# Feed-forward products from the unscaled residual, and GpSimd's past taps paced by weight units, in a two-layer retention and convolution decoder step

## The chip, the cores and the metric

One core of one Trainium2 chip runs the whole program. The metric is the device time of one execution in microseconds. The engines are TensorE (PE; its weight loads PEld), VectorE (DVE), ScalarE (ACT), GpSimd (POOL) and SyncE (SP), each with its own instruction queue; they meet at semaphores.

## What is computed

Two trunk layers over 320 tokens (256 of a prompt, 8 x 8 of a decoding batch), width 1024, all in fp32:

```python
h = rms_norm(x, g_mix_pre); proj = h @ w_in          # q, k, v, g_ret, ca, cb, ga, gb
# retention: rope(q, k), chunkwise state, layer norm, silu(g_ret) * o, @ w_ret_out
# convolution: u = ca * sigmoid(cb), depthwise, 31 taps, layer norm, silu, @ w_conv_out
merged = sigmoid(ga + b_ga) * y_ret + sigmoid(gb + b_gb) * y_conv
x = x + rms_norm(merged @ w_o, g_mix_post)
h2 = rms_norm(x, g_ffn_pre)
f = (silu(h2 @ w_ffn_gate) * (h2 @ w_ffn_up)) @ w_ffn_down
x = x + rms_norm(f, g_ffn_post)
```

`rms_norm` divides each token by the root of its mean square. The new states of retention and convolution are outputs too.

## The kernel before

Tokens lie along the free axis, features on the partitions (8 tiles of 128x320). Each product is made in units: a unit is 8 tiles of 128x128 weights, 512 KB, one output tile of 128x320. fp32 is split in two fp32r halves: ScalarE copies the weights to `whi` and VectorE makes `wlo = w - whi` (L1025, the helper `lower`, called by `split`), and TensorE does three products per tile (L415 to L417 in `unit`, `bank` in PSUM). A layer has 180 units: 16 of the convolution inputs (CIN), 4 heads of 12, 8 of the gate gb, 24 of ga and the retention output (RET), 8 convolution output, 8 `w_o`, 44 feed-forward gate and up alternating (GU, from U_GU = 112), 24 down. Four ring slots hold weights; `split(l, u)` prepares unit u + 3 (AHEAD = 3), once unit u - 1 is done.

The order on each engine is written out by hand:

- `normalised` (VectorE, L1038) makes h = x times gain times rstd, ScalarE copies the upper half `hhi` (`halves_of_h`, L894), VectorE the lower half `hlo`. `first_units` (TensorE, L435 to L437) then does the first three units of a stage together, K-step by K-step, as the halves come: 8 steps of 9 matmuls. `rsqrt` (ScalarE) is Ln (L774) then Exp (L781) of the mean square, which TensorE sums over the partitions with `ones_d` (`stat`, L468; L449 and L454 for squares of products). `keep_clock(n)` issues n products whose result nobody reads (L444).
- `log_exp_table` (L770) loads by name a table of ScalarE that has both Ln and Exp. Other loads are placed by the compiler.
- The depthwise convolution of the prompt is 124 taps of two VectorE instructions each (128x256, L1056 for a pair's first tap, L1060 for the others), spread by hand over units: CIN_TAPS, FIRST_HEAD_TAPS, HEAD_TAPS, GB_TAPS, RET_TAPS say how many taps follow the split of each unit, by layer.
- The sample's convolution is GpSimd's: `past_taps` (L272 product, L275 addition, 30 taps, 60 instructions; here 128x512 or less) over the stored rows, `new_taps` (L289, L291). Its queue is: past taps of layer 0, store of cs_out, new taps, then the state stores and loads of each head (L299, L257), later the past taps of layer 1 during layer 0's feed-forward, from the third gated product on (FFN_FIRST).
- A head's retention is done in two parts: `early` in its own units, `late` in the next head's (or gb's) units 0 to 7, between the K-steps (j, k). UPDATE_AT holds the eight places of the state update products (L580, two at a time), QUERY_AT those of the state reading products (L563), which wait for the state's load. `update` (VectorE, L1091) takes a product's bank into the state; `aux_free` lets a product reuse one of three banks only when the product three before it has been read. So the products at (5, 5) wait for update 12, the first of the two that follow the split of unit 5.
- `post` (VectorE) copies the product, waits for the rstd, then adds it to x in four groups of two tiles (L1374, L1376); ScalarE squares each tile of x (L992) for the next norm.
- In the feed-forward, ScalarE takes the sigmoid of the gate bank (L793), VectorE multiplies bank and sigmoid (L1393) and then with the up bank (L1399), ScalarE and VectorE make the halves for the down product (L999, L1025).

## Time and profile before

| | us |
|---|---|
| median of 3 runs | 1566.42 (1566.14 to 1571.51) |
| the profiled execution | 1567.79 |
| its span | 1566.0 |
| TensorE busy | 1513.0 (97%), 9840 instructions |
| VectorE busy | 1107.8 (71%) |
| ScalarE busy | 674.4 (43%) |
| GpSimd busy | 287.5 (18%) |
| chain that ended last, by engine | PE 79%, DVE 14%, ACT 3% |

The mean granted clock of TensorE is 0.99 of 2.4 GHz. TensorE's busy time contains the fillers of `keep_clock`, and matmuls overlap, so a busy TensorE can still hold time that isn't needed. A matmul of the main product is listed with 0.31 us, and the next one starts 0.15 us behind it.

### The profile page before, as it was taken

To read this page: it belongs to the slowest core of one execution; us is meant where nothing else is said; L and a number is where in the kernel's file an instruction comes from. 1 tells how busy PE (TensorE), PEld (TensorE's weight loads), DVE (VectorE), ACT (ScalarE), POOL (GpSimd) and SP (SyncE) were. 2 spreads that over 40 slices of the span, in tenths; PEclk is the share of its full clock that TensorE was granted. 3 is DMA by queue.
4 is the path that set the end of the run, shared out by engine and by line. 5 is a ranking of instruction groups with operands and counts; after the bars stand their busy time and mean duration, and the time that the engine had idled before them with its cause. 6 is when DMAs were issued, how large, how long until landed. Compare 5 with 4: busy or idle time off the path is not lost.

```text
span 1566.0 us, 25591 instructions
## 1 busy us (share of the span) xinstructions
PE 1513.0 (97%) x9840; PEld 1399.5 (89%) x9840; DVE 1107.8 (71%) x1735; ACT 674.4 (43%) x993; POOL 287.5 (18%) x257
## 2 busy tenths in 40 slices
PE   6999999999999999999999999999999999999997
PEld 5997878687999999999999978788789998999997
DVE  6699978977757567654456988989685665655544
ACT  4333434355355354334343334344464544443433
POOL 6974000011110029910000400101002000000000
PEclk9999999999999999999999999999999999999999
DMA  6554755647444434444444555658554342544443
GB/s 255 175 193 158 275 201 216 229 175 256 135 149 147 157 110 146 157 148 158 156 152 158 195 207 216 245 183 311 180 184 161 135 148 68 175 148 148 155 156 117
DMA packets 64540, 275.48 MB, mean 176 GB/s; under 512 B 7232, under 2 KB 7232, under 8 KB 55232
## 3 DMA queue, kind: packets, MB, share of 16 engines
q1 hardware_dynamic: 52560, 192.17, 35.8%
q0 software_dynamic: 11888, 82.04, 13.9%
q8 instruction: 62, 1.02, 0.3%
q14 instruction: 30, 0.25, 0.0%
HBM read 230.30 MB, written 43.89 MB: 175 GB/s over the span
## 4 chain that ended last, share of the span: by engine, by line
PE 79%; DVE 14%; ACT 3%; issue 1%; POOL 1%; DVEq 0%; ACTq 0%
PE bank L415 23%; PE bank L417 22%; PE bank L416 22%; DVE acc L1060 4%; DVE wlo L1025 3%; PE bank L602 2%; DVE state L1091 1%; PE bank L580 1%; DVE tmp L1080 1%; PE bank L563 1%; PE bank L516 1%; DVE x L1376 1%; ACT L770 1%; DVE tmp L1374 1%; PE bank L545 1%
## 5 line engine op out<-in xcount | busy, mean ns | idle before, releaser
L415 PE MATMUL bank<-hhi,whi 128*128 128x320 f32 x2016 | 654.5, 325 | 1.6 <-DVE wlo L1025 1.6
L417 PE MATMUL bank<-hhi,wlo 128*128 128x320 f32 x2016 | 625.2, 310 | 0.0
L416 PE MATMUL bank<-hlo,whi 128*128 128x320 f32 x2016 | 624.8, 310 | 0.0
L1025 DVE TENSOR_TENSOR wlo<-wring,whi 128x1024 fp32r<-128x1024 f32 x363 | 470.4, 1297 | 217.0 <-ACT whi L763 194.5
L415 PEld LDWEIGHTS bank<-hhi,whi 128*128 128x128 f32 x2016 | 380.8, 189 | 33.6 <-issue 29.3
L416 PEld LDWEIGHTS bank<-hlo,whi 128*128 128x128 f32 x2016 | 381.1, 189 | 8.6 <-issue 7.7
L763 ACT ACTIVATE whi<-wring 128x1024 fp32r<-128x1024 f32 x264 | 278.1, 1055 | 241.4 <-PE bank L417 239.1
L417 PEld LDWEIGHTS bank<-hhi,wlo 128*128 128x128 f32 x2016 | 380.5, 189 | 0.0
L1060 DVE SCALAR_TENSOR_TENSOR acc<-up,par,acc 128x256 f32<-128x256 f32 x480 | 211.1, 507 | 0.2
L789 ACT ACTIVATE whi<-wring 128x1024 fp32r<-128x1024 f32 x96 | 101.2, 1054 | 73.3 <-PE bank L417 72.0
L793 ACT ACTIVATE sig<-bank 128x320 f32<-128x320 f32 x92 | 40.2, 437 | 199.6 <-PE bank L417 187.2
L415 PE MATMUL bank<-fhi,whi 128*128 128x320 f32 x352 | 110.4, 314 | 0.0
L417 PE MATMUL bank<-fhi,wlo 128*128 128x320 f32 x352 | 108.5, 308 | 0.0
L416 PE MATMUL bank<-flo,whi 128*128 128x320 f32 x352 | 108.5, 308 | 0.0
L1091 DVE SCALAR_TENSOR_TENSOR state<-state,con,bank 128x512 f32<-128x512 f32 x128 | 89.8, 744 | 11.4 <-PE bank L580 10.3
L299 POOL DMA_DIRECT2D rs_out<-state x32 | 17.3, 541 | 390.1 <-DVE state L1091 390.1
L392 POOL DMA_DIRECT2D par<-params x2 | 1.2, 576 | 465.0 <-DVE acc L1368 465.0
L415 PE MATMUL bank<-ghi,whi 128*128 128x320 f32 x256 | 78.8, 308 | 2.4 <-DVE glo L1025 2.4
L416 PE MATMUL bank<-glo,whi 128*128 128x320 f32 x256 | 78.8, 308 | 0.0
L417 PE MATMUL bank<-ghi,wlo 128*128 128x320 f32 x256 | 78.7, 307 | 0.0
L1393 DVE TENSOR_TENSOR tmp<-bank,sig 128x320 f32<-128x320 f32 x44 | 21.6, 492 | 70.5 <-ACT sig L793 70.5
L416 PEld LDWEIGHTS bank<-flo,whi 128*128 128x128 f32 x352 | 66.1, 188 | 0.6
(157 smaller groups left out, 1948.1 us busy)
## 6 DMA issues: line engine op xcount, KB each, us to landing
wring<-w SPq DMA_DIRECT2D x364, 512.0 KB, 3.7
state<-r_in POOLq DMA_DIRECT2D x32, 1024.0 KB, 7.6
rs_out<-state POOLq DMA_DIRECT2D x32, 1024.0 KB, 5.0
rp_out<-pst POOLq DMA_DIRECT2D x8, 512.0 KB, 8.4
us<-c_in POOLq DMA_DIRECT2D x2, 1216.0 KB, 5.7
cs_out<-us POOLq DMA_DIRECT2D x2, 1216.0 KB, 9.4
cp_out<-up POOLq DMA_DIRECT2D x2, 1144.0 KB, 5.9
con<-consts POOLq DMA_DIRECT2D x1, 1420.0 KB, 9.3
```

Source lines behind the costliest of these rows:

```text
L299: pool.dma_start(rs_out[H * QUADS + q], state[q % 2][:, :, :]).then_inc(r_stored[q % 2], 16)
L415: pe.matmul(bank[g][:, 0:T], whi[j][:, k, :], hi, start=start and k == 0, stop=False)
L416: pe.matmul(bank[g][:, 0:T], whi[j][:, k, :], lo, start=False, stop=False)
L417: mm = pe.matmul(bank[g][:, 0:T], wlo[j][:, k, :], hi, start=False, stop=stop and k == n - 1)
L602: mm = pe.matmul(aux[pos % 3][:, :], kdec[:, c, d * P:(d + 1) * P], vtok[:, c, :], start=(c == 0), stop=(c == 1))
L763: act.activation(whi[s][:, :, :], wring[s][:, :, :], ACT.Copy).then_inc(hi_done, 1)
L789: act.activation(whi[s][:, :, :], wring[s][:, :, :], ACT.Copy).then_inc(hi_done, 1)
L793: act.activation(dst, src, ACT.Sigmoid).then_inc(sig_done, 1)
L1025: return dve.tensor_tensor(dst, value, hi.bitcast(F32), ALU.subtract)
L1060: dve.scalar_tensor_tensor(out=out, in0=src, scalar=tap, in1=out, op0=ALU.mult, op1=ALU.add).then_inc(conv_step, 1)
L1091: dve.scalar_tensor_tensor(out=st, in0=st, scalar=con[:, ds(hd + C_CD, 1)], in1=aux[pos % 3][:, :], op0=ALU.mult, op1=ALU.add).then_inc(dv ...
L1393: dve.tensor_tensor(tmp[:, n % 4, :], bank[b][:, 0:T], sig[:, n % 4, :], ALU.mult).then_inc(ffn_step, 1)
```

## The change

1. Feed-forward entrance: the units work on x times gain, without rstd. ScalarE makes `hhi` straight from x as its groups come (MIX_GROUPS, two of one tile, three of two), VectorE `hlo` (`x_low`). The mean square runs meanwhile: squares are added in halves (`add_squares`), and TensorE sums four in place of eight, inside `first_units`. The split of unit U_GU stands ahead of the wait for the mixer's rstd, that of U_GU + 1 behind the feed-forward's. keep_clock(20) and keep_clock(12) become one keep_clock(12).
2. In each feed-forward step VectorE multiplies the gate bank by rstd, ScalarE takes Silu of that, VectorE multiplies the up bank by rstd and then both with each other.
3. Start of layer 0: squares of x are added in halves, four sums in place of eight, 18 fillers before them; the named table load goes; GpSimd's first past taps wait for all eight `hlo`.
4. GpSimd's past taps of layer 1 wait, each, for a unit: the first for 20 units of the stage, the others spread over 42.
5. `first_updates` puts the updates 0, 1, 8, 9, 12, 13 and the token statistics ahead of the split of their unit; UPDATE_AT (4, 7) becomes (4, 5).
6. Tap lists of layer 0: 8 taps in CIN (0 before), 10 in head 0 (16), 23 in head 1 (27), 21 in gb (20), 8 in RET (7).

```diff
-CIN_TAPS = (0, 2)
-FIRST_HEAD_TAPS = ((1, 2, 1, 1, 1, 2, 2, 1, 1, 1, 1, 2), (2, 2, 2, 2, 2, 2, 2, 1, 1, 1, 1, 2))
-HEAD_TAPS = ((7, 0, 3, 0, 4, 1, 5, 4, 3, 0, 0, 0), (7, 0, 3, 0, 3, 1, 4, 3, 2, 0, 0, 0))
-GB_TAPS = ((6, 0, 3, 3, 3, 1, 4, 0), (5, 0, 3, 3, 2, 1, 3, 0))
-RET_TAPS = ((1, 2, 2, 2, 0, 0), (1, 2, 2, 1, 0, 0))
-FFN_FIRST = 3
+CIN_TAPS = ((1, 1, 1, 1, 2, 2), (2, 2, 2, 2, 2, 2))
+FIRST_HEAD_TAPS = ((1, 1, 1, 1, 1, 1, 1, 1, 1, 0, 0, 1), (2, 2, 2, 2, 2, 2, 2, 1, 1, 1, 1, 2))
+HEAD_TAPS = ((5, 0, 3, 0, 3, 1, 5, 3, 3, 0, 0, 0), (7, 0, 3, 0, 4, 1, 5, 4, 3, 0, 0, 0), (7, 0, 3, 0, 3, 1, 4, 3, 2, 0, 0, 0))
+GB_TAPS = ((6, 0, 3, 3, 3, 2, 4, 0), (5, 0, 3, 3, 2, 1, 3, 0))
+RET_TAPS = ((2, 2, 2, 2, 0, 0), (1, 2, 2, 1, 0, 0))
+FFN_FIRST, TAP_UNITS = 20, 42
-UPDATE_AT = ((1, 0), (1, 3), (1, 5), (1, 7), (4, 3), (4, 7), (5, 3), (5, 5))
+UPDATE_AT = ((1, 0), (1, 3), (1, 5), (1, 7), (4, 3), (4, 5), (5, 3), (5, 5))
...
+                    if paced:
+
+                        pool.wait_ge(unit_done, (l - 1) * UNITS + (U_GU + FFN_FIRST + k * TAP_UNITS // PAD))
...
+                    pool.wait_ge(h_ready, KT)
                     past_taps(0, past0, stap, par[:, G_CB:G_CW], par[:, G_CW:NPAR])
...
+                if l == 0:
+                    keep_clock(18)
+                    for k in (0, 1, 4, 5):
+                        pe.wait_ge(x_halves, k // 4 + 1)
+                        mm = pe.matmul(X[:, 0:T], ones_d[:, :], sq8[:, k, :], start=(k == 0), stop=(k == 5))
...
-                keep_clock(20)
...
+                def both_halves(k):
+
+                    if k == 5:
+                        half_mean(0)
+                    if k == 6:
+                        half_mean(1).then_inc(stat_done, 1)
+
+                first_units(l, U_GU // RING, lambda k: h_read(l, 8 + k), between=both_halves)
...
-            log_exp_table()
...
+                split(l, U_GU)
                 act.wait_ge(stat_done, l * STATS + (ST_POST + 1))
                 rsqrt(l, X[:, 0:T], ST_POST, RS_POST)
...
+                for i, (k0, n) in enumerate(MIX_GROUPS):
+                    act.wait_ge(post_step, l * POSTS + (2 * i + 2))
+                    for k in range(k0, k0 + n):
+                        act.activation(hhi[:, k, :], x[:, k, :], ACT.Copy, scale=g_(G_FFNPRE + k)).then_inc(h_hi, 1)
+                    for k in range(k0, k0 + n):
+                        act.activation(sq8[:, k, :], x[:, k, :], ACT.Square).then_inc(sq_done, 1)
...
-                    gemm(l, U_GU + 2 * n)
-                    sigmoid(sig[:, n % 4, :], bank[(2 * n) % 4][:, 0:T])
+                    act.wait_ge(ffn_step, l * (2 * FT) + (2 * n + 1))
+                    act.activation(sig[:, n % 4, :], sig[:, n % 4, :], ACT.Silu).then_inc(sig_done, 1)
...
+            def first_updates(l, hd, j):
+
                 if j in (1, 4, 5):
                     q = (1, 4, 5).index(j)
+                    for i in range(2):
                         update(l, hd, (0, 8, 12)[q] + i)
+                if j == 5:
+                    token_stats(l, hd, 1, range(2, 3))
+
+                    dve.wait_ge(bn_done, (l * HEADS + hd) * 3 + 3)
+                if j == 6:
+                    token_shift(l, hd, 1, slice(2, 3))
...
+                for i, (k, n) in enumerate(MIX_GROUPS):
+                    x_group(l, 2 * i, k, n)
+                    for low in ((), (0,), (1,), (2, 3), (4, 5, 6, 7))[i]:
+                        if low == 7:
+                            add_squares(0)
+                            add_squares(1)
+                        x_low(low)
...
+                    dve.tensor_tensor(sig[:, n % 4, :], bank[b][:, 0:T], rstd[:, :], ALU.mult).then_inc(ffn_step, 1)
...
+                    dve.tensor_tensor(tmp[:, n % 4, :], bank[b + 1][:, 0:T], rstd[:, :], ALU.mult).then_inc(ffn_up, 1)
+                    dve.wait_ge(ffn_up, l * FT + (n + 1))
+                    dve.wait_ge(sig_done, l * SIGS + (SIG_GATE + n + 1))
+                    dve.tensor_tensor(tmp[:, n % 4, :], tmp[:, n % 4, :], sig[:, n % 4, :], ALU.mult).then_inc(ffn_step, 1)
```

## Rows read from the trace of the kernel before

**Rows 1.** Table by stages (stretch, length; busy us of PE, PEld, DVE, ACT, POOL; clock, DMA).

```profile
45.00:130.00 85.00, 84.95 (x583) 84.39 (x582) 66.69 (x88) 31.70 (x46) 71.94 (x56) 1.00 0.52 181
...
200.00:269.00 69.00, 66.32 (x407) 54.49 (x406) 60.44 (x119) 29.02 (x47) 4.80 (x9) 0.98 0.60 221
...
540.50:565.00 24.50, 23.21 (x155) 20.86 (x154) 15.12 (x26) 12.15 (x25) 0.00 (x0) 1.00 0.12 42
565.00:710.00 145.00, 145.00 (x990) 145.00 (x990) 94.26 (x108) 59.76 (x86) 90.42 (x60) 1.00 0.45 152
```

**Rows 2.** Waits of TensorE: who waited for whom, us, times, longest.

```profile
PE bank L580 <- DVE state L1091: 16.2, 17, 2.1
```

**Rows 3.** Table by stages, the half-clock stretches of layer 0's heads.

```profile
173.90:177.30 3.40, 3.40 (x15) 3.40 (x15) 2.79 (x8) 1.84 (x5) 1.05 (x2) 0.50 0.42 163
...
310.40:317.20 6.80, 6.56 (x24) 6.16 (x25) 5.55 (x12) 2.58 (x5) 1.05 (x2) 0.50 0.63 212
```

**Rows 4.** Timeline of TensorE (start, us, engine, line, operation, idle before): products of state updates.

```profile
242.02 0.69 PE L580 MATMUL bank<-vst,kst 32*128 32x512 f32 x2 [2.09 <-DVE state L1091]
...
1012.32 0.50 PE L580 MATMUL bank<-vst,kst 32*128 32x512 f32 x2 [1.30 <-DVE state L1091]
```

**Rows 5.** Timeline of all engines, start of layer 0; two rows of VectorE's.

```profile
9.76 1.28 ACT L770 ACT_TABLE_LOAD   x1
...
11.05 2.95 ACT L913 ACTIVATE whi<-wring 128x1024 fp32r<-128x1024 f32 x3
...
14.97 0.53 ACT L774 ACTIVATE lnv<-bank,eps 128x320 f32<-128x320 f32 x1 [0.97 <-PE bank L468]
...
21.08 1.56 DVE L1043 SCALAR_TENSOR_TENSOR acc<-x,par,rstd 128x320 f32<-128x320 f32 x1
...
21.30 0.60 PE L435 MATMUL bank<-hhi,whi 128*128 128x320 f32 x1 [3.69 <-DVE hlo L1025]
...
89.68 2.34 DVE L1056 TENSOR_SCALAR acc<-up,par 128x256 f32<-128x256 f32 x2
...
105.95 1.67 DVE L1080 TENSOR_TENSOR tmp<-bank,con 128x320 f32<-128x320 f32 x4
```

**Rows 6.** Timeline at the feed-forward's entrance, layer 0.

```profile
543.08 0.83 DVE L1374 TENSOR_TENSOR tmp<-acc,rstd 128x640 f32<-128x640 f32 x1 [1.37 <-ACT rstd L781]
...
552.62 1.48 DVE L1043 SCALAR_TENSOR_TENSOR acc<-x,par,rstd 128x320 f32<-128x320 f32 x3 [3.07 <-ACT rstd L781]
...
554.64 0.38 PE L435 MATMUL bank<-hhi,whi 128*128 128x320 f32 x1 [0.52 <-DVE hlo L1025]
```

**Rows 7.** Timeline of VectorE in head 2, units 4 and 5.

```profile
234.11 2.80 DVE L1091 SCALAR_TENSOR_TENSOR state<-state,con,bank 128x512 f32<-128x512 f32 x4
236.83 3.25 DVE L1060 SCALAR_TENSOR_TENSOR acc<-up,par,acc 128x256 f32<-128x256 f32 x8
240.00 1.22 DVE L1025 TENSOR_TENSOR wlo<-wring,whi 128x1024 fp32r<-128x1024 f32 x1
241.13 1.41 DVE L1091 SCALAR_TENSOR_TENSOR state<-state,con,bank 128x512 f32<-128x512 f32 x2
```

**Rows 8.** Timelines of GpSimd and TensorE, head 0 to head 1; DMA issues there.

```profile
105.90 0.53 POOL L360 DMA_DIRECT2D cs_out<-us  x1
...
133.93 1.33 POOL L291 TENSOR_TENSOR acc<-us,stap 128x512 f32<-128x512 f32 x1
...
148.39 0.59 POOL L299 DMA_DIRECT2D rs_out<-state  x1 [13.14 <-DVE state L1091]
...
153.64 0.54 POOL L257 DMA_DIRECT2D state<-r_in  x1 [1.75 <-DMA rs_out<-state]
...
state<-r_in POOLq DMA_DIRECT2D x2, 1024.0 KB, 7.7
...
161.97 1.05 PE L563 MATMUL bank<-state,qz 128*16 128x512 f32 x8
```

**Rows 9.** Timeline of TensorE at the mean of the convolution, layer 0.

```profile
415.33 0.81 PE L695 MATMUL bank<-pairs,ones_d 128*128 128x320 f32 x2 [1.59 <-POOL pairs L371]
```

More of the change, by code:

```diff
@@ L261, in window, with past_taps @@
                 return buf[:, :, :, t0:t0 + n]
-            def past_taps(l, past, ptap, bias, weights):
+            def past_taps(l, past, ptap, bias, weights, paced=False):
                 weights = weights.rearrange("p (n k) -> p n k", n=KT)
@@ L439, in first_units @@
                             mm.then_inc(unit_done, 1)
+                    if between is not None:
+                        between(k)
             def keep_clock(n):
@@ L1208, in head @@
             def head(l, hd, first):
-                taps = (FIRST_HEAD_TAPS if first else HEAD_TAPS)[l]
+                taps = FIRST_HEAD_TAPS[l] if first else HEAD_TAPS[2 if l else min(hd - 1, 1)]
                 for j in range(HEAD_UNITS):
-                    if j == 1 and not first:
-                        update(l, hd - 1, 0)
-                        update(l, hd - 1, 1)
-                    if j == 6 and not first:
-                        token_shift(l, hd - 1, 1, slice(2, 3))
+                    if not first:
+                        first_updates(l, hd - 1, j)
                     split(l, U_HEAD + j, hd)
@@ L1282, in _ @@
                 for n in range(KT):
-                    if n == 1:
-                        update(l, last, 0)
-                        update(l, last, 1)
-                    if n == 6:
-                        token_shift(l, last, 1, slice(2, 3))
+                    first_updates(l, last, n)
                     split(l, U_GB + n)
@@ L1368, in post @@
                         dve.tensor_scalar(acc[:, n, :], bank[n % 4][:, 0:T], g_(gain + n), None, ALU.mult).then_inc(y_copied, 1)
+                    if sub == 0:
+                        split(l, U_GU)
                     dve.wait_ge(rstd_done, l * RSTDS + (rs + 1))
                     dve.wait_ge(y_copied, l * 16 + (8 * sub + 8))
-                    scale = rstd[:, :].rearrange("p (o t) -> p o t", o=1).to_broadcast([P, 2, T])
-                    for n in range(0, KT, 2):
-                        y = tmp[:, n % 4:n % 4 + 2, :]
-                        dve.tensor_tensor(y, acc[:, n:n + 2, :], scale, ALU.mult).then_inc(post_step, 1)
-                        dve.wait_ge(post_step, l * POSTS + (8 * sub + n + 1))
-                        dve.tensor_tensor(x[:, n:n + 2, :], x[:, n:n + 2, :], y, ALU.add).then_inc(post_step, 1)
@@ L1378, in _, with x_group @@
-                post(0, RS_POST, SQ_POST, G_MIXPOST, U_WO, 1)
-                dve.wait_ge(post_step, l * POSTS + 8)
-                normalised(l, 1, RS_FFN, G_FFNPRE)
+                def x_group(l, step, k, n):
+                    y = tmp[:, k % 4:k % 4 + n, :]
+                    scale = rstd[:, :].rearrange("p (o t) -> p o t", o=1).to_broadcast([P, n, T])
+                    dve.tensor_tensor(y, acc[:, k:k + n, :], scale, ALU.mult).then_inc(post_step, 1)
+                    dve.wait_ge(post_step, l * POSTS + (step + 1))
+                    dve.tensor_tensor(x[:, k:k + n, :], x[:, k:k + n, :], y, ALU.add).then_inc(post_step, 1)
@@ new lines, in x_low, with add_squares @@
+                def x_low(k):
+                    dve.wait_ge(h_hi, l * 16 + (8 + k + 1))
+                    dve.scalar_tensor_tensor(out=hlo[:, k, :], in0=x[:, k, :], scalar=g_(G_FFNPRE + k), in1=hhi[:, k, :].bitcast(F32),
+                                             op0=ALU.mult, op1=ALU.subtract).then_inc(h_ready, 1)
+                def add_squares(i):
+                    dve.wait_ge(sq_done, l * SQS + (SQ_FFN + 4 * i + 4))
+                    dve.tensor_tensor(sq8[:, 4 * i:4 * i + 2, :], sq8[:, 4 * i:4 * i + 2, :], sq8[:, 4 * i + 2:4 * i + 4, :],
+                                      ALU.add).then_inc(sq_halves, 1)
```

101 lines of the change are left out of this document (56 added, 45 removed).

## The prediction

> **What bounds the kernel now.** I read the table by stages first. TensorE is the bound nearly everywhere: it is busy for 84.95 of 85 us in the convolution inputs and the first head, and for all 145 us of a feed-forward stretch [rows 1]. So an edit pays only where TensorE stands still, runs fillers, or runs at its lower clock. The reader is to look for the stretches in which its busy time is short of the stretch: a head loses 2.7 of 69 us, the 24.5 us between the output projection and the first feed-forward units lose 1.3 and hide fillers besides [rows 1]. The waits of TensorE say who ends them: 16.2 us in 17 waits are waits of L580 (the state update product) for the VectorE update L1091 [rows 2]. Then the clock: three stretches of the first layer's heads stand at 0.50, which is 1.2 GHz, two of 3.4 us and one of 6.8 us (the first and the last are shown); in the last a matmul takes 6.56 / 24 = 0.27 us [rows 3], against 145 / 990 = 0.147 in the feed-forward [rows 1]. The timeline ties the second of them to a wait: L580 at 242.02 has stood 2.09 us for VectorE, just where the clock falls [rows 4]. The like wait of the second layer is 1.30 us, and the clock stays up behind it [rows 4].
>
> **The part at the start of layer 0.** Before, GpSimd's 60 past-tap operations run beside `normalised`; a VectorE multiply of 128x320 takes 1.56 us there [rows 5] and 0.49 us without GpSimd (1.48 for three) [rows 6]. The change lets GpSimd begin only when all eight `hlo` are made. With eight steps of about 0.87 us (two such operations, each overlapping its successor a little) the first 96 K-steps of TensorE are then no longer fed by VectorE but by its own rate. The first of them starts 2.0 us behind the rstd, as in the feed-forward (552.62 to 554.64) [rows 6], in place of 5.2 us behind it (rstd 1.1 us after Ln's start at 14.97, first product at 21.30) [rows 5], and the 72 matmuls take 72 x 0.147 = 10.6 us in place of some 18 before (21.30 and eight steps of two operations of 1.56 and like length, less their overlap): the first units end some 10 us sooner, if the rstd comes at its old time. Does it? The 18 fillers and the halved sum bring the sum from 14.9 to about 12, but ScalarE has its three copies (2.95 us behind 9.76, where squares end) in front of Ln in any case, so Ln starts at 12.7 at best [rows 5]. The preload of the table is taken out, and Ln and Exp still need a table: with none to load rstd stands at 13.8, with one load of 1.28 at 15.0, with two (one for Ln, one for Exp, as no line now names a table that has both) at 16.3, against 16.1 before. I take the two loads, since the program asked for that table by name wherever both functions follow each other; so the rstd itself gains nothing.
>
> The trace shows 1.28 us for a load, and the next instruction (11.05) starts directly behind it [rows 5]. The Trainium skill (ScalarE: Activation LUTs, What ACT_TABLE_LOAD costs) adds a drain of 1.38 us to each switch of set, 2.66 us in all; by it the two loads would put the rstd 2.8 us later than I take it. The row shows no such drain, so it counts 1.28 here.
>
> The 10 us don't last. GpSimd's 60 operations are now all in front of the convolution inputs and head 0, where VectorE has also got 8 taps in place of none (6 fewer in head 0, net +2). There VectorE and GpSimd hold each other up: a pair of tap instructions that is 0.8 us alone (3.25 for eight) [rows 7] took 2.34 us at 89.68 [rows 5]. From the last `hlo` (about 24) to the second rope of head 0, which TensorE waits for, VectorE has 20 splits x 1.13, 8 gates of bank times sigmoid at about 0.6, 12 taps x 0.8 and some 3.2 of rope = 40 us of its own. A GpSimd operation in between adds 0.77 (2.34 against 0.8, halved) to 1.07 us (1.56 against 0.49), say 0.95, and 24 to 47 of them meet one (half or all of those that fit): 88 to 109. Before, that rope started at 105.95 [rows 5], just in time for TensorE; TensorE by itself now wants the rope's banks 19 units of 3.52 us behind its 28.6, at 95.5. With rope times of 88 to 109, head 0 ends between 9 us sooner and 3 us later. I take no gain, because VectorE is now loaded throughout, so that nearly each of its operations meets one of GpSimd's.
>
> Behind this is GpSimd's own queue: past taps, the cs_out store (105.90), new taps to 135.3, and only then the state stores and loads [rows 8]. Before, it stood waiting for the store at 148.39. 60 operations from 23.6 at the 1.5 to 1.75 us that contention makes of them end at 114 to 129 instead of 105; 30 us later the stores can start, and the load they release lands 12.9 us behind the store (148.39 to the load at 153.64, and 7.7) while TensorE asks for it 13.6 us behind it (161.97) [rows 8]. So the state comes between on time and 8 us late; I take 2 us. **Start and first head: +2 us, from -9 to +10.**
>
> **Heads.** `first_updates` sets two state updates ahead of the weight split of units 4 and 5, and the product at (4,7) moves to (4,5). The product at (5,5) needs update 12. Before, VectorE does four updates (234.11), eight tap instructions (236.83), the split (240.00, 1.13 to the next), then update 12 (241.13) [rows 7]. Now update 12 comes one split sooner: 1.13 us. Queued behind it is the split itself, whose weights are wanted three units (over 10 us) later, so its delay costs nothing; if VectorE were already 7 us behind, it would cost all of its wait. There are eight such places (three heads and the gb stage of each layer). One tap less at unit 4 of head 1 is 0.8 us more: 8 x 1.13 + 0.8 = 9.8, of 16.2 that there is to get [rows 2]; in the last stage of layer 1 part of it is not there. **-9.5 us, from -5 to -12.**
>
> **Clock.** The idle time at (5,5) in heads 2 and 3 of layer 0 falls from 2.09 to about 1.3 us, after which the trace of layer 1 shows no fall [rows 4]. In 13.6 us at 0.27 in place of 0.147 per matmul TensorE loses 13.6 x 0.45 = 6.1 us [rows 3]. I take 5, since new idle time in head 0 and at its followers may cost one fall. **-5 us, from 0 to -6.**
>
> **Convolution sums.** RET_TAPS and GB_TAPS of layer 0 carry one tap more each; the mean's product L695 already stands 1.59 us for GpSimd's sum of them [rows 9]. One tap of two instructions, 0.8 us: **+0.8** (0 to +2).
>
> **Feed-forward entrance, twice.** Before: rstd of the mixer 543.08, four groups of product and addition at 0.83 each, squares, eight products of the sum, Ln, Exp, normalisation, first product 554.64 [rows 6]. Now hhi = x times gain is made while the groups come. ScalarE's and VectorE's split of unit U_GU lie in front: the first is hidden by the sum's own path, the second ends 0.2 us behind the old start, so groups start at 543.3. Two narrow groups (2 x 0.93), one low part 0.5: first product at 545.7. Then a group of two costs 1.6 and low parts 0.5, so that K-steps 1 and 2 (1.32 us each) wait 0.75 each; from K-step 3 on TensorE is behind and the rest is hidden. The 72 matmuls 10.6, idle 1.5, and four sum products of two passes now inside the units, 4 x 0.54 + 0.5 = 2.6: end 560.4, against 554.64 + 10.6 = 565.2. That is 4.75 us, 9.5 for both layers, less 0.1. Next late is the rstd that the bank readers want: sum at 559.3, Ln, Exp 560.5, split, 1.28 load, VectorE's gate scale at 563, with unit 4 wanted at 564. Just hidden; without that cover each us late costs one. If the waits in the K-steps drop the clock, 3.4 to 6.8 us at 1.2 GHz cost 1.5 to 3 us a layer. **-9.4 us, from -3 to -11.**
>
> In steady state, VectorE gets one 0.49 us operation more per pair of units (gate x rstd, up x rstd, product in place of two): 44 in all, 21.6 us. A pair of units is 7.05 us, and VectorE's is then 2 x 1.13 + 4 x 0.45 = 4.1 and the ping-pong with ScalarE (scale, Silu, half, copy, split, up, product, split) 5.4 us, 6.5 with GpSimd between; hidden, as now [rows 1]. Pacing the 30 taps over 42 units takes contention from a stretch that loses nothing and puts it into the down stage, where it loses nothing either: 0. If VectorE fell more than two units behind, it would cost what the cycle has over 7.05.
>
> The trace shows the 1.56 us for operations that read two SBUF tensors. The Trainium skill (GPSIMD Engine Reference, Key points) says just that: contention with VectorE's instructions that have two SBUF inputs or a 2-port mode. By it the two scalings, one input of which is a bank, run free of GpSimd; were they hit too, the cycle would be 7.4 us and the second half of layer 0's feed-forward lose up to 8 us. The page sides with zero; no row here has such a scaling beside GpSimd in the feed-forward.
>
> **The sum.** +2 - 9.5 - 5 + 0.8 - 9.4 = -21.1 us. The profiled execution took 1567.8 (span 1566.0), so its like would take 1546.7; the median shown is 1.4 lower, which gives 1545.3. I say 1546.
>
> **Rivals.**
> - *The start pays too*: VectorE catches up in head 0 and the stores aren't late, so 8 us of the 10 stay. For: GpSimd has idle stretches of VectorE to run in. Against: the second rope was the point that TensorE just met before. 1546 - 10 = 1536. Chance 0.15.
> - *The waits only move*: u8 to u12 are held by the products before them, or the clock falls at the new gaps. Then the heads give 4 and the clock 0: 1546 + 10.5 = 1556. Chance 0.17.
> - *The stage entrance is all that counts* and head 0's lateness takes what the heads give: -9.4 + 10 - 5 = -4: 1562. Chance 0.09.
> - *GpSimd's queue, slower*: its taps meet a VectorE that is never idle. If each of its operations (0.95) has to let a split (1.13) pass, with the gap it takes 2.15 us; 60 of them from 23.6 end at 152, the stores start at 182, the state lands at 195, 33 us late for head 1, where the reordered updates hold up the splits too. The rest gives 23: 1566 + 10 = 1576. It decides from an end of the past taps at 142 on, where the lateness is 23. Against: VectorE must idle where TensorE bounds. Chance 0.04.
> - *It doesn't do what it says*: a table load in each feed-forward step, because Silu's table lacks the copy. 44 x 1.28 on ScalarE per layer would still fit in 7 us: no change of sign. 0.01.
>
> The forecast itself has 0.54. Its own range is 1539 to 1553; with bounds and rivals the range is 1535 to 1560. A measurement of this kernel tells about 0.5% (8 us, below 1558.6) from no change: faster 0.87, same 0.09, slower 0.04.
>
> **What would show it.** L435's first products at about 18 (layer 0) and 9 us sooner than before at both feed-forwards. L580's waits for L1091 from 16.2 to near 7. No half clock between 170 and 320. Past taps ending at 114 to 129 and PE L563 waiting a little for r_in once. ACT table loads in front of both Ln and Exp near 13 and 15. Wrong it would be if TensorE waits for wlo in the feed-forward, or if head 0 starts 10 us sooner and stays so.

## The result and the profile after

The changed kernel takes 1546.86 us (median; 1545.82 to 1548.0) where the kernel before takes 1566.68 on the same chip: a ratio of 0.987, with an interval of 0.9845 to 0.9888. The forecast was 1546. Its span is 1546.2 us against 1566.0. Below stand, for the changed kernel, the page's lines of busy times and of the chain that ended last, the waits of TensorE (who waited for whom, us, times, longest) and the table by stages (columns as in [rows 1]). Its line numbers are shifted: L592, L1125 and L1094 are the state product, the state update and the taps (before L580, L1091, L1060); L445 and L425 the first and the other weight units (L435, L415); L1059 is `lower` (L1025), L1114 the first rotary products (L1080).

```profile
PE 1500.5 (97%) x9772; PEld 1392.2 (90%) x9772; DVE 1143.6 (74%) x1773; ACT 675.4 (44%) x994; POOL 272.0 (18%) x257
PE 80%; DVE 14%; ACT 3%; issue 1%; POOL 1%; DMA 0%; DVEq 0%; ACTq 0%
```

```profile
PE bank L425 <- DVE tmp L1114: 7.8, 2, 4.3
PE bank L592 <- DVE state L1125: 4.8, 10, 1.1
PE bank L445 <- DVE hlo L1059: 4.2, 2, 3.7
...
PE bank L714 <- POOL pairs L382: 3.8, 2, 3.2
```

```profile
45.00:130.00 85.00, 77.19 (x507) 76.36 (x506) 78.06 (x82) 27.71 (x39) 70.18 (x57) 0.96 0.45 154
190.00:267.00 77.00, 75.89 (x474) 63.99 (x474) 67.33 (x133) 32.55 (x53) 4.79 (x9) 0.98 0.60 214
539.50:554.00 14.50, 13.30 (x81) 12.18 (x82) 9.55 (x16) 6.95 (x17) 0.00 (x0) 1.00 0.05 18
554.00:698.00 144.00, 144.00 (x984) 144.00 (x983) 108.70 (x127) 61.85 (x87) 46.93 (x35) 1.00 0.48 152
```

The waits for the state have shrunk from 16.2 us [rows 2] to 4.8. A new wait heads the list: 7.8 us for the rotary products. It lies in the stretch 45 to 130, where TensorE had next to no idle time [rows 1] and now has 7.8 us.

To see where the 19.8 us of span come from, I took from each kernel's timeline of TensorE the start of the last product of a stage, and subtracted that of the kernel before. All kernels of this study stand in one table (us; layer 0 up to the bar). Each row is one execution, the profiled one, and differences of up to 3 us in it can be stretches at half clock that come in one execution and not in another (last section):

| kernel | conv. input | head 0 | gb | RET | first 3 FF units | &#124; gb | conv. output | first 3 FF units, and end |
|---|---|---|---|---|---|---|---|---|
| changed | -9.9 | +1.2 | -9.1 | -6.0 | -11.3 | -16.4 | -14.5 | -19.8 |
| a_no_start | -0.3 | -0.1 | -9.7 | -9.7 | -15.0 | -19.3 | -19.2 | -24.5 |
| a_no_heads | -9.0 | +0.5 | -2.8 | -1.2 | -6.5 | -6.8 | -6.5 | -11.7 |
| a_ffn_alone | -0.1 | +0.1 | 0.0 | 0.0 | -5.3 | -5.6 | -5.6 | -10.9 |
| a_burst | -8.6 | +0.4 | -11.8 | -8.7 | -13.9 | -17.8 | -16.2 | -21.5 |
| a_small_taps | -8.7 | -9.0 | -20.5 | -17.5 | -22.8 | -27.9 | -27.5 | -32.8 |
| a_rope_first | -9.7 | -0.7 | -11.9 | -8.7 | -14.0 | -17.7 | -17.4 | -22.7 |
| b_ret | -10.1 | +2.6 | -10.6 | -10.6 | -15.9 | -20.9 | -20.5 | -25.8 |
| a_combo | -13.5 | -3.5 | -13.2 | -13.2 | -18.6 | -23.7 | -23.3 | -28.6 |
| c_later_taps | -13.5 | -7.8 | -11.2 | -11.2 | -16.5 | -21.3 | -20.9 | -25.4 |
| b_gate_off | +0.3 | +2.0 | -10.3 | -7.0 | -12.3 | -16.3 | -15.9 | -21.2 |
| c_update47 | -9.9 | +1.2 | -9.5 | -6.3 | -11.6 | -16.1 | -15.7 | -21.0 |
| d_spread | -13.5 | -13.8 | -21.9 | -21.9 | -27.2 | -31.8 | -31.4 | -36.7 |

The first row reads as a sum: the start and head 0 cost 1.2, the heads up to gb give 10.3 in layer 0 and 5.1 in layer 1, each feed-forward entrance 5.3, the retention output's stage takes 3.2 and layer 1's stages up to the convolution output take 1.9 back.

**The start.** Timelines of the changed kernel: ScalarE, TensorE's first product, GpSimd's first past tap.

```profile
12.37 1.28 ACT L805 ACT_TABLE_LOAD   x1
13.67 0.53 ACT L805 ACTIVATE lnv<-bank,eps 128x320 f32<-128x320 f32 x1
14.21 1.28 ACT L812 ACT_TABLE_LOAD   x1
15.51 0.47 ACT L812 ACTIVATE rstd<-lnv 128x320 f32<-128x320 f32 x1
...
18.11 0.38 PE L445 MATMUL bank<-hhi,whi 128*128 128x320 f32 x1 [3.66 <-DVE hlo L1059]
...
23.27 1.06 POOL L281 TENSOR_TENSOR past<-us,par 128x512 f32<-128x512 f32 x1 [11.56 <-DVE hlo L1059]
```

Two loads stand in front of Ln and Exp, and the first units still end 9 to 10 us sooner, as the table's first column has it.

**Head 0 of layer 0.** VectorE's timeline, the first matmuls behind TensorE's two waits, and the table by stages behind each.

```profile
88.57 2.08 DVE L1059 TENSOR_TENSOR wlo<-wring,whi 128x1024 fp32r<-128x1024 f32 x1
90.58 2.71 DVE L1094 SCALAR_TENSOR_TENSOR acc<-up,par,acc 128x256 f32<-128x256 f32 x2
93.21 1.67 DVE L1114 TENSOR_TENSOR tmp<-bank,con 128x320 f32<-128x320 f32 x4
...
94.54 0.54 PE L425 MATMUL bank<-hhi,whi 128*128 128x320 f32 x1 [4.28 <-DVE tmp L1114]
...
106.92 0.41 PE L425 MATMUL bank<-hhi,whi 128*128 128x320 f32 x1 [3.54 <-DVE tmp L1114]
```

```profile
94.70:98.10 3.40, 3.40 (x14) 3.40 (x15) 3.40 (x4) 0.00 (x0) 3.24 (x3) 0.50 0.00 0
108.30:111.70 3.40, 3.40 (x15) 3.40 (x14) 3.40 (x5) 0.00 (x0) 3.01 (x6) 0.50 0.10 17
```

Here the start's gain is lost: 4.4 and 3.7 us by the starts of the matmuls, and the clock falls to 1.2 GHz for 3.4 us behind each wait (0.50 in the table), which costs 1.5 us a time. That is the 11.1 us between the first two columns.

**The retention output's first units.** GpSimd's last sum of the convolution, TensorE's product that waits for it, and the stretch behind it in the table by stages.

```profile
406.06 1.72 POOL L382 TENSOR_TENSOR pairs<-pairs 128x320 f32<-128x320 f32 x1
...
407.83 0.81 PE L714 MATMUL bank<-pairs,ones_d 128*128 128x320 f32 x2 [3.22 <-POOL pairs L382]
```

```profile
408.70:412.10 3.40, 3.40 (x15) 3.40 (x14) 0.00 (x0) 0.00 (x0) 0.00 (x0) 0.50 0.42 140
```

The wait was 1.59 us [rows 9]. It is 1.6 us longer, and RET loses 3.2 us in all against gb; the other 1.5 are the half clock. a_no_heads has the same longer wait and no half clock there, and loses 1.6 (-2.8 to -1.2).

**The feed-forward's entrance.** Timeline of the changed kernel.

```profile
539.80 0.38 PE L445 MATMUL bank<-hhi,whi 128*128 128x320 f32 x1 [1.13 <-DVE hlo L1426]
...
541.77 0.41 PE L445 MATMUL bank<-hhi,whi 128*128 128x320 f32 x1 [0.41 <-DVE hlo L1426]
...
554.88 1.28 ACT L1039 ACT_TABLE_LOAD   x1
...
556.04 0.48 DVE L1455 TENSOR_TENSOR sig<-bank,rstd 128x320 f32<-128x320 f32 x1
```

The layer stood 5.99 us ahead at its output projection; with that added the first product is at 545.8 in the time of the kernel before, where the prediction has 545.7.

### The profile page after: what moved, and what is told of

It is laid out like the page before. It is cut to its first block, busy times and chain, and to the rows that moved or that the text cites. A ratio compares the mean times of both kernels' runs of the same rounds, so it can differ in the third digit from the quotient of the medians.

```text
span 1546.2 us, 25486 instructions
## 1 busy us (share of the span) xinstructions
PE 1500.5 (97%) x9772; PEld 1392.2 (90%) x9772; DVE 1143.6 (74%) x1773; ACT 675.4 (44%) x994; POOL 272.0 (18%) x257
## 4 chain that ended last, share of the span: by engine, by line
PE 80%; DVE 14%; ACT 3%; issue 1%; POOL 1%; DMA 0%; DVEq 0%; ACTq 0%
PE bank L425 23%; PE bank L427 22%; PE bank L426 22%; DVE acc L1094 5%; DVE wlo L1059 2%; PE bank L614 2%; DVE state L1125 2%; PE bank L592 1%; PE bank L575 1%; DVE tmp L1114 1%; PE bank L445 1%; PE bank L528 1%; PE bank L447 1%; PE bank L446 1%; PE bank L557 1%
## 5 line engine op out<-in xcount | busy, mean ns | idle before, releaser
L425 PE MATMUL bank<-hhi,whi 128*128 128x320 f32 x2016 | 655.4, 325 | 8.7 <-DVE tmp L1114 7.8
L1059 DVE TENSOR_TENSOR wlo<-wring,whi 128x1024 fp32r<-128x1024 f32 x363 | 479.6, 1323 | 192.3 <-ACT whi L794 178.1
L425 PEld LDWEIGHTS bank<-hhi,whi 128*128 128x128 f32 x2016 | 381.2, 189 | 40.3 <-issue 29.3
L1094 DVE SCALAR_TENSOR_TENSOR acc<-up,par,acc 128x256 f32<-128x256 f32 x480 | 226.4, 536 | 0.2
L425 PE MATMUL bank<-fhi,whi 128*128 128x320 f32 x352 | 110.5, 314 | 0.0
L1125 DVE SCALAR_TENSOR_TENSOR state<-state,con,bank 128x512 f32<-128x512 f32 x128 | 89.4, 739 | 11.2 <-PE bank L592 10.3
L425 PE MATMUL bank<-ghi,whi 128*128 128x320 f32 x256 | 78.9, 308 | 2.4 <-DVE glo L1059 2.4
L1039 ACT ACTIVATE sig<-sig 128x320 f32<-128x320 f32 x44 | 20.8, 472 | 123.9 <-DVE sig L1455 123.9
L425 PEld LDWEIGHTS bank<-fhi,whi 128*128 128x128 f32 x352 | 66.1, 188 | 0.6
L427 PEld LDWEIGHTS bank<-fhi,wlo 128*128 128x128 f32 x352 | 66.1, 188 | 0.0
```

Of the source, the lines that this page charges most:

```text
L425: pe.matmul(bank[g][:, 0:T], whi[j][:, k, :], hi, start=start and k == 0, stop=False)
L427: mm = pe.matmul(bank[g][:, 0:T], wlo[j][:, k, :], hi, start=False, stop=stop and k == n - 1)
L1039: act.activation(sig[:, n % 4, :], sig[:, n % 4, :], ACT.Silu).then_inc(sig_done, 1)
L1059: return dve.tensor_tensor(dst, value, hi.bitcast(F32), ALU.subtract)
L1094: dve.scalar_tensor_tensor(out=out, in0=src, scalar=tap, in1=out, op0=ALU.mult, op1=ALU.add).then_inc(conv_step, 1)
L1125: dve.scalar_tensor_tensor(out=st, in0=st, scalar=con[:, ds(hd + C_CD, 1)], in1=aux[pos % 3][:, :], op0=ALU.mult, op1=ALU.add).then_inc(dv ...
```

## The experiments

### Parts undone

**a_no_start**: the start of layer 0, and all tap lists of layer 0, as before.

```diff
-CIN_TAPS = ((1, 1, 1, 1, 2, 2), ...   # and the other four lists of layer 0
+CIN_TAPS = ((0, 0, 0, 0, 0, 0), ...
-                    pool.wait_ge(h_ready, KT)       # ahead of past_taps(0, ...)
-                if l == 0: keep_clock(18); four sums  # and VectorE's x_halves
+            log_exp_table()                          # by name again
```

> The changed kernel with its start undone: GpSimd's past taps of layer 0 begin at once, the eight sums, the table load by name and the tap lists of layer 0 are those of before. Theory (the start's 9.9 us are eaten in head 0 by VectorE and GpSimd hindering each other): the first three units end at 39.3 as before, but the end of head 0 stands at 132, about 1 us sooner than in the changed kernel (133.3), and the wait of the convolution's mean falls from 3.2 to 1.6 us, so that the whole takes 1544 us, 3 less than the changed kernel. Rival (the start pays): 10 us more than the changed kernel, 1557.

**a_no_heads**: VectorE's order of updates and `(4, 7)` as before (`updates` does all, `first_updates` only what stood ahead of the split at units 1 and 6).

> The changed kernel with the old order of state updates and the product at (4, 7). Theory: each of eight places loses 1.1 us again, and the clock falls behind waits of 2.1 us in layer 0: 9 us of waits and 2 to 5 us of clock, 1558 us. L580's waits for the update stand at 14 to 16 us. Rival (the waits only move, the gain in heads comes from the tap lists): 1549 us.

**a_ffn_alone**: both undone, so only the feed-forward's part is left.

> The feed-forward part of the change alone (unscaled products, Silu, paced taps), start and heads as before. Theory: each feed-forward entrance gives 5.3 us, the rest nothing: 10.6 us less than before, 1556 us. Rival (the entrance's gain is lost in the steps, where VectorE has one operation more and ScalarE waits for it): 1560 us or more, with the end of the gate and up units less than 4 us sooner than before.

**a_burst**: the layer 1 taps on GpSimd in one burst.

```diff
-  pool.wait_ge(unit_done, (l - 1) * UNITS + (U_GU + FFN_FIRST + k * TAP_UNITS // PAD))
+  pool.wait_ge(unit_done, (l - 1) * UNITS + (U_GU + 7))
```

> The changed kernel, but GpSimd's past taps of layer 1 all follow each other from the seventh unit of the feed-forward on. Theory: TensorE never waits there, so pacing is worth nothing: 1547 us, within 1.5 us of the changed kernel. Rival (pacing is what makes the longer steps fit): VectorE falls behind in the units 10 to 35 of the stage, TensorE waits for weights, 1552 us or more.

Measured, in this order: 1542.71 (ratio 0.983, 0.9812 to 0.9849), 1559.24 (0.9941, 0.9922 to 0.9959), 1557.09 (0.9919, 0.9898 to 0.994) and 1546.65 us (0.9861, 0.9842 to 0.988).

So the start, with its tap lists, costs 4 us by the medians and 6 by the ratios: without it the kernel is faster. Without the reordered updates the kernel is 12 us slower by the medians; its profiled execution, the fastest of its four, shows 8 us of span. The cleaner pair is a_ffn_alone and a_no_start, measured on one chip and with the same tap lists, the ones of before: they differ in the updates alone, and these give 14.4 us, 9.5 of the span in layer 0's heads and gb, clock included, and some 4 in layer 1's. The feed-forward's part alone gives 5.3 at each entrance, and in the table next to nothing elsewhere (0.3 in layer 1's heads). Pacing GpSimd is worth about nothing: the burst loses 1.1 us in the gate and up stage (-13.9 to -12.9), and the medians are the same. The waits for the state sort the kernels the same way, first without the heads' part, then the feed-forward's alone, then without the start:

```profile
PE bank L592 <- DVE state L1125: 14.0, 16, 2.1
```

```profile
PE bank L591 <- DVE state L1119: 15.5, 17, 2.1
```

```profile
PE bank L591 <- DVE state L1119: 6.2, 10, 1.1
```

a_no_start also loses nothing in the retention output's stage (-9.7, -9.7), so the 3.2 us there went with the start, or with the tap lists that were undone beside it.

### Why the start doesn't pay

**a_small_taps**: GpSimd's past taps of layer 0 behind the first made small. The kernel so leaves out most of the past's share in the decoding batch's convolution, and its time serves the argument alone.

```diff
-                    n = min(DS, PAD - k)
+                    n = min(DS, PAD - k) if paced or k == 0 else 1
```

> The changed kernel with GpSimd's layer 0 past taps after the first cut from up to 8 tokens to one (64 elements instead of 512); this leaves out most of the decode stream's past convolution sum in layer 0 and moves nothing else. Theory: the start's 9.9 us, which are there at the end of the convolution input product, are lost in head 0 because the past taps lie beside VectorE up to 113.5 us and draw out the rotary work by which two units wait (4.44 and 3.70 us). Then both losses go, head 0 ends 8 to 10 us sooner than in the kernel before, and the whole is 1538 us (1535 to 1541). Rival: head 0 is bound by VectorE's own work, whoever shares its port. Then a loss of at least 5 us stays near 94 and 107 us and the whole is 1545 to 1547.

**a_rope_first**: in head 0 of layer 0, at units 1 and 3, `rope` ahead of `conv_taps`.

> The changed kernel with one thing swapped: in head 0 of layer 0, at units 1 and 3, the rotary products stand ahead of that unit's convolution tap on VectorE (a contended tap pair takes some 2.5 us there). Theory: the two losses of 4.44 and 3.70 us are the time by which VectorE is late with the rotary sum; each falls by about 2.5 us less what the clock does with a shorter idle, whole 1542 us (1540 to 1544). Rival: VectorE is late by a debt from further ahead, which the swap only moves to the next split; then the two losses shrink and others of the same size stand at the units behind them, whole 1545 to 1548.

**b_gate_off**: GpSimd's wait for the eight tiles taken out (`pool.wait_ge(h_ready, KT)`).

> The changed kernel without the wait that holds GpSimd's layer 0 past taps back until the eight normalised tiles are ready; nothing else. Theory: the taps begin near 16 us and end 8 us sooner (105 us), so VectorE runs head 0's second half alone, but its normalised tiles take 1.5 us a step instead of 0.5; the first products lose some 4 us more and head 0 some 6 us less, whole 1545 us (1542 to 1547). Rival: the gate is what makes the start pay; without it the first products fall back to the times of before the change and head 0 still loses its 8 us, whole 1550 to 1554.

Measured: 1535.62 (0.9794, 0.9776 to 0.9811), 1544.7 (0.9855, 0.9833 to 0.9877), 1545.97 (0.9859, 0.9843 to 0.9874).

With small taps nothing is lost in head 0: it ends 9.0 us sooner, and all that follows with it (1535 to 1541 expected). So it is what GpSimd's taps add to VectorE's operations that eats the start. VectorE and GpSimd in the same head, first the timeline with small taps, then the table by stages of the changed kernel and of the small taps, 76 to 90 and 90 to 110 us:

```profile
83.24 0.87 DVE L1094 SCALAR_TENSOR_TENSOR acc<-up,par,acc 128x256 f32<-128x256 f32 x2
84.46 1.69 DVE L1114 TENSOR_TENSOR tmp<-bank,con 128x320 f32<-128x320 f32 x4 [0.35 <-PE bank L427]
...
86.86 1.22 DVE L1059 TENSOR_TENSOR wlo<-wring,whi 128x1024 fp32r<-128x1024 f32 x1
```

```profile
76.00:90.00 14.00, 14.00 (x98) 14.00 (x96) 14.00 (x12) 4.25 (x4) 13.29 (x10) 1.00 0.34 113
90.00:110.00 20.00, 12.19 (x66) 11.66 (x66) 20.00 (x22) 3.82 (x5) 18.75 (x17) 0.87 0.25 80
```

```profile
76.00:90.00 14.00, 14.00 (x98) 14.00 (x97) 12.22 (x23) 4.25 (x4) 3.18 (x6) 1.00 0.88 310
90.00:110.00 20.00, 20.00 (x140) 19.99 (x140) 20.00 (x23) 9.27 (x17) 13.85 (x13) 1.00 0.41 139
```

A tap (two instructions) takes 2.71 us beside GpSimd and 0.87 without, a split 2.08 against 1.22. In the first stretch the changed kernel's VectorE issues 12 instructions in 14.00 busy us, the other 23 in 12.22. It has no idle time left and falls behind, until TensorE stands for the banks that the rotary products have yet to read. The rotary products, with one input in a bank, take the same 1.67 and 1.69.

Putting the rotary products first only moved the loss, as the rival had it: 1.9, 4.0 and 1.4 us are lost near 92, 100 and 110, now for the rotary products and twice for `wlo`. It is a debt of VectorE's work and not, in the main, a matter of the order within a unit: head 0 ends 1.9 us sooner than in the changed kernel, and the time lies just under the rival's 1545 to 1548. Without the gate, GpSimd's past taps end 10 us sooner (103.8 in place of 113.6), head 0 loses only one wait of 1.5 us, but the first product comes at 21.2 behind a wait of 6.7, and of the start nothing is left (+0.3). What the gate gives at the start it takes in head 0. The time is the one expected, 1545, but by other amounts: the start loses 10 us where 4 were expected, as the rival said, and head 0 loses 1.7 and not the rival's 8.

### The tap in the retention output's stage

**b_ret**: only layer 0's later tap lists as before.

```diff
-HEAD_TAPS = ((5, 0, 3, 0, 3, 1, 5, 3, 3, 0, 0, 0), ...
-GB_TAPS = ((6, 0, 3, 3, 3, 2, 4, 0), ...
-RET_TAPS = ((2, 2, 2, 2, 0, 0), ...
+HEAD_TAPS = ((5, 0, 3, 0, 3, 1, 6, 4, 3, 0, 0, 0), ...
+GB_TAPS = ((6, 0, 3, 3, 3, 1, 4, 0), ...
+RET_TAPS = ((1, 2, 2, 2, 0, 0), ...
```

> The changed kernel with layer 0's tap lists from the gate product on as in the kernel before (one tap of the gate product and one of the gated sum's stage moved back ahead, into the second and following heads: 6 and 4 instead of 5 and 3 at the units 6 and 7). Theory: the 3.2 us that the changed kernel loses between the gated sum and the down end of the convolution output (a wait of 1.6 us longer for the sum over pairs, and a half clock of 3.4 us at 408.7) come from the tap put there, which makes VectorE's split and GpSimd's sum run at the same time; without it they don't come, whole 1543.5 us (1542 to 1545). Rival: the stage is late because the heads before it were quicker than GpSimd's and ScalarE's part of the gated sum; then the wait stays 3 us and the whole is 1546 to 1548.

Measured: 1541.18 us (0.9827, 0.981 to 0.9844), 5.7 below the changed kernel. GpSimd's sum and TensorE's product there:

```profile
403.82 0.86 POOL L382 TENSOR_TENSOR pairs<-pairs 128x320 f32<-128x320 f32 x1
...
404.74 0.81 PE L714 MATMUL bank<-pairs,ones_d 128*128 128x320 f32 x2 [1.58 <-POOL pairs L382]
```

The sum takes 0.86 in place of 1.72 and the product waits 1.58 in place of 3.22; RET loses nothing against gb (-10.6, -10.6). The waits of all kernels bear it out: the seven with the tap there have 3.8 us in the row of this product, the longest 3.2, and the seven without it (the kernel before among them) 2.1 and 1.6; six of the former have a half clock behind the wait. That is 3.2 of the 6.0 us of span; this run also has no half clock at 238 and none in layer 1 at 1231, which the changed kernel has (1.5 each), and loses 1.4 more in head 0; some 1.2 are spread over smaller waits. These two falls can't be put down to the lists: a_burst, with the changed kernel's lists, has none at 238, and a_rope_first and c_update47, with the same lists, none in layer 1. So the trace shows 3.2 us as the lists' own, and why the median lies below the 1542 to 1545 expected stays open. Since a_no_start (1542.71) has these lists too, the start by itself gives at most a microsecond or two, and by the ratios (0.9827 and 0.983) nothing.

### The order of the updates

**c_update47**: TensorE's place of before, VectorE's new order.

```diff
-UPDATE_AT = (..., (4, 3), (4, 5), (5, 3), (5, 5))
+UPDATE_AT = (..., (4, 3), (4, 7), (5, 3), (5, 5))
```

> The changed kernel with one of PE's eight state updates at its place of before (after the unit 7 of the fourth group instead of after the unit 5), VectorE's new order kept. Theory: of the heads' gain the order of VectorE's updates carries all, since it is what cuts the wait for the state from 2.1 to 1.1 us; PE's own place gives nothing, whole 1547 us (1545 to 1549), half clocks as in the changed kernel. Rival: the two belong together, and with PE's place undone a wait of some 2 us comes back in each of the seven heads behind the first, or a half clock at 310, whole 1553 to 1559.

Measured: 1547.93 us (0.9882, 0.9867 to 0.9897), the same as the changed kernel within its interval. The heads and gb of layer 1 still give 4.5 us (-11.6 to -16.1) of 5.1, and no wait for the state is over 1.5 us. VectorE's order carries nearly all of it, as the first theory had it. The half clocks did not stay as expected: there is none near 238 and one of 3.4 us at 305, near the rival's 310, and with falls that come and go this one decides nothing.

### Towards a better kernel

**a_combo**: a_rope_first and b_ret, and `log_exp_table()` ahead of the squares.

> The changed kernel with the rotary products first in head 0 of layer 0, the later tap lists as before the change, and the logarithm and exponential table loaded by name ahead of the squares, so that neither Ln nor Exp loads one behind the sum of squares. By the theories above the three add: 2.5 us from one or two table loads of 1.28 us, 4.5 us from the rotary work and 3 us from the gated sum's stage, whole 1537 us (1534 to 1540). Rival: what the start gains is eaten by the same queue of VectorE in head 0 whatever its order; then the table gives nothing and the whole is 1543 to 1546.

**c_later_taps**: against a_combo, seven taps moved back: two out of the convolution input and five out of head 0's first six units; five go to head 0's later units and two to head 1. (The expectation counts head 1 from the changed kernel's list.)

```diff
-CIN_TAPS = ((1, 1, 1, 1, 2, 2), ...
-FIRST_HEAD_TAPS = ((1, 1, 1, 1, 1, 1, 1, 1, 1, 0, 0, 1), ...
-HEAD_TAPS = ((5, 0, 3, 0, 3, 1, 6, 4, 3, 0, 0, 0), ...
+CIN_TAPS = ((1, 1, 1, 1, 1, 1), ...
+FIRST_HEAD_TAPS = ((0, 0, 0, 0, 0, 1, 2, 2, 2, 1, 1, 1), ...
+HEAD_TAPS = ((7, 0, 3, 0, 4, 1, 5, 4, 3, 0, 0, 0), ...
```

> The last kernel of the call before (rotary products first, later tap lists of before, table by name) with six more of layer 0's taps moved out of the stretch that VectorE shares with GpSimd: two from the convolution input's last units and four from head 0's first units; four of these go to head 1, which then has the list of heads 2 and 3, two to head 0's own later units. Theory: VectorE has no idle time from 52 to 120 us there, so head 0's losses (2.37, 4.06 and 1.29 us) are a debt of work, and 6 taps of some 2.5 us pay it off; head 0 loses at most 1 us and the whole is 1531 us (1529 to 1534). Rival: the taps only come back later, in head 1, where each lies ahead of the split at a half-precision unit; then head 1 loses what head 0 gains and the whole is 1536 to 1539.

Measured: 1538.22 (0.9809, 0.9791 to 0.9827) and 1541.6 us (0.9837, 0.9824 to 0.9851). The table by name brought the convolution input 3.7 us forward against a_rope_first (-13.5, -9.7), more than the two loads of 1.28: ScalarE's timeline of a_combo has no load between the copies and Ln.

```profile
12.43 0.51 ACT L805 ACTIVATE lnv<-bank,eps 128x320 f32<-128x320 f32 x1
12.97 0.47 ACT L812 ACTIVATE rstd<-lnv 128x320 f32<-128x320 f32 x1
...
16.09 0.38 PE L445 MATMUL bank<-hhi,whi 128*128 128x320 f32 x1 [1.48 <-DVE hlo L1060]
```

The first product comes 2.0 us sooner than in the changed kernel and 2.2 sooner than in a_rope_first, and this run has no half clock near 20 us, which both of these have (1.5 us).

c_later_taps missed, and more went back than the rival said. Head 0's rotary products no longer made anyone wait, but TensorE's timeline shows the debt twice, behind the taps at the head's end and behind head 1's seven:

```profile
117.32 0.66 PE L505 MATMUL bank<-con,qkv 128*128 128x128 f32 x2 [3.27 <-DVE kdec L1214]
...
141.62 0.79 PE L592 MATMUL bank<-vst,kst 32*128 32x512 f32 x2 [5.11 <-DVE state L1126]
```

The seven taps ahead of the first update take VectorE 11.98 us beside GpSimd's new taps, more than there is room for, once TensorE arrives sooner. So the last kernel spares both places:

**d_spread**, against a_combo:

```diff
+CIN_TAPS = ((1, 1, 1, 1, 1, 1), ...
+FIRST_HEAD_TAPS = ((0, 0, 0, 0, 0, 0, 1, 1, 1, 1, 3, 3), ...
+HEAD_TAPS = ((5, 0, 3, 0, 3, 1, 6, 4, 3, 0, 0, 0), (7, 0, 3, 0, 4, 1, 5, 4, 3, 0, 0, 1), ...
```

> The combined kernel (rotary products first, later tap lists of before, table by name) with layer 0's taps spread anew: none in head 0's first six units (there were six) and two fewer at the end of the convolution input; six in head 0's last two units, where GpSimd's past taps are over, two more at other units there, head 1's list kept as it was, and one more in the last unit of each of the heads 2 and 3. Theory: a tap costs VectorE some 2.5 us while GpSimd's past taps run and 0.9 behind them, and head 1 has no room for more in its first unit; so head 0's losses of 7.7 us go, nothing comes back in head 1, and the whole is 1532 us (1529 to 1535), below every kernel so far. Rival: PE's 3.5 us a unit leave VectorE no room in head 0 even without taps, or the wait only moves to the state in head 1, as with the version before; then 3 to 6 us are lost behind 115 us and the whole is 1537 to 1542.

Measured: 1532.5 us (0.978, 0.9767 to 0.9794), the fastest kernel of the study that computes the whole: 2.2% below the kernel before, 0.9% below the changed one (by the two ratios). Its waits:

```profile
PE bank L592 <- DVE state L1126: 6.9, 8, 3.1
```

No row for the rotary products, and head 0 ends 13.8 us sooner than before. Of that 3.8 go back at the start of head 1: the five taps of its first unit, beside GpSimd's new taps, take 7.42 us, the state product behind them waits 3.11, and the clock falls for 3.4 us. a_combo loses 0.4 there. So the theory's 1532 us came, but its "nothing comes back in head 1" did not: the loss that the rival named is there, in the size that it gave (3 to 6 us). At the end of head 1 the kernel is 13.2 us ahead, because the half clock that the kernel before has in that head [rows 3] is gone.

## Why the prediction was right, point by point

- **Start and first head, +2: measured +1.2.** The steps hold. Two loads, rstd ready at 15.98 (said 16.3), first product 18.1 (about 18), first units 9 to 10 us sooner (10), and head 0 takes it all, because VectorE is loaded throughout. The past taps end at 113.6, just short of the 114 to 129 given: 61 operations in 90.3 us are 1.48 each, under the 1.5 I began from. The term for a late state was wrong: GpSimd's stores waited 7.12 us for VectorE, not VectorE's state for GpSimd, and TensorE's waits have no row of L575 for the load. What made up for it was the clock, two falls that I had not priced in this term. Right in size, then, by luck: two errors of 2 and 3 us stand against each other.
- **Heads -9.5 and clock -5: measured -10.3 and -5.1 in the two layers.** In layer 1, where no clock fell before, the four places give 1.2, 1.6, 1.2 and 1.1 us, against 1.13 each. In layer 0 the first place gives 4.1 us and head 3's 3.8, each with a half-clock stretch that is gone. But a_no_heads gains 3.3 us there without the reordering, for one half-clock stretch of 3.4 us fewer and the tap less at unit 4 of head 1 among others; so the reordering itself is some 7 of the 10.3, or 9.5 with the tap lists of before (a_no_start against a_ffn_alone). "No half clock between 170 and 320" was wrong: one of 3.4 us stands at 238, behind a wait of 1.11 us.
- **Convolution sums +0.8: measured +3.2.** The mechanism was right and the size was not. I priced a tap at its time alone, 0.8 us; it also pushed VectorE's split beside GpSimd's last sum (0.86 to 1.72: in the changed kernel the split runs from 405.80 to 407.07 and the sum from 406.06 on, in b_ret the split starts at 404.34 and the sum has ended by 404.68), and behind the longer wait the clock fell. Of the 3.2, 1.6 are wait and the rest clock. The term for this step was short by 2.4 us.
- **Feed-forward entrances -4.7 each: measured -5.3 and -5.3.** Two idle times were lost in the K-steps, 0.58 and 0.64 by the matmuls' starts (said 0.75 each), and the three units took 14.2 us from the first product (said 14.7). The clock stayed up through both. The bank readers' rstd was just hidden: the table load and the scale at 556.04 hold TensorE up nowhere: it has no wait in that stretch.
- **Steady feed-forward 0, pacing 0: measured 0 and about -1 in the trace.** TensorE is busy for 144.00 of 144 us, VectorE for 108.70, against 94.26 of 145 [rows 1].
- **Not in the sum: +1.9 in layer 1's convolution output**, of which up to 0.4 is there in the versions without a fall, and 1.5 a fall of the clock at 1231.3 that a_no_start doesn't show.

The terms miss by -0.8, -0.9, +2.4, -1.2 and, for what the sum left out, +1.9 us. Together that is 1.4, and so the forecast lies closer to the measured time than its parts do to theirs: the mechanisms were mostly right, the last microseconds are luck.

The feed-forward's operations bear on the passage on contention. VectorE's groups of the changed kernel in that stage:

```profile
L1059 DVE TENSOR_TENSOR wlo<-wring,whi 128x1024 fp32r<-128x1024 f32 x42 | 60.0, 1428 | 12.1 <-ACT whi L794 11.6
L1059 DVE TENSOR_TENSOR flo<-tmp,fhi 128x320 fp32r<-128x320 f32 x21 | 18.7, 890 | 18.8 <-ACT fhi L1032 18.8
L1466 DVE TENSOR_TENSOR tmp<-tmp,sig 128x320 f32<-128x320 f32 x21 | 13.8, 656 | 0.9 <-ACT sig L1039 0.2
L1455 DVE TENSOR_TENSOR sig<-bank,rstd 128x320 f32<-128x320 f32 x22 | 10.7, 485 | 8.3 <-PE bank L427 8.3
L1463 DVE TENSOR_TENSOR tmp<-bank,rstd 128x320 f32<-128x320 f32 x21 | 10.1, 483 | 0.0
```

The scalings, which read a bank, take 485 and 483 ns; the product of two SBUF tensors of the same size takes 656 on average, and the lower half 890. The averages mix two cases. Where a GpSimd operation lies beside more than half of it, a product takes 875 ns on average, a lower half 1420 and a split 2093; elsewhere they take 492, 492 and 1220. The scalings take 484 and 485 ns beside GpSimd and elsewhere. By the Trainium skill (GPSIMD Engine Reference, Key points) the engines contend when VectorE has two SBUF inputs; the trace agrees, and the case in which the scalings are hit too did not come.

The load's price is settled as well. The first load starts at 12.37 and Ln at 13.67, 1.30 behind it, the second at 14.21 and Exp at 15.51. The Trainium skill (ScalarE: Activation LUTs, What ACT_TABLE_LOAD costs) has a drain of 1.38 us besides; no such gap stands in these rows, and the measurement decides.

## What to carry over

When one engine's first work is brought forward, ask what the engine behind it has left: here 10 us at the start were worth nothing until the work of VectorE in the contended stretch was cut, and 13.5 us at the start (with the table by name) were worth 13 behind head 1 once it was. Price an operation beside GpSimd at its contended time (a tap 2.7 us, not 0.9), and place movable work where GpSimd is silent. And where an update releases a product three places on, set it ahead of the split that is not wanted yet: a change of order alone, worth about 1.3 us at each of layer 1's four places.
